# Delta rule of a two-block transformer: row spreads as one rounded product, pairs formed one ahead, the recurrence in halves of four heads

## The reference

```python
beta  = sigmoid(beta_logit)                       # per head and token
log_g = -exp(a_log) * softplus(decay_logit + dt_bias)
gam   = cumsum(log_g)                             # inside a chunk
decay = exp(gam[:, None] - gam[None, :])          # lower triangle, else 0
lower = strictly_lower(beta[:, None] * (k @ k.T) * decay)
T     = inverse(I + lower)
u_base, w_state = T @ (beta * v), T @ (beta * exp(gam) * k)
p_intra = (q @ k.T) * decay
q_dec, k_dec, g_tot = q * exp(gam), k * exp(gam[-1] - gam), exp(gam[-1])
for each chunk, with the state s of each head:
    u = u_base - w_state @ s
    o = q_dec @ s + p_intra @ u
    s = g_tot * s + k_dec.T @ u
```

## Time and profile before

| | us |
|---|---|
| median of 3 runs | 4046.73 |
| profiled execution, its time | 4045.87 |
| its span on the core | 4044.1 |
| PE busy (share of the span) | 3848.6 (95%) |
| DVE busy | 2100.2 (52%) |
| ACT busy | 1354.6 (33%) |

### The profile page before, as it was taken

One profiled execution on the slowest core, in us unless ns is written; L12 is line 12 of the kernel. 1 busy time (PEld: TensorE's weight loads), 2 busy tenths in 40 slices (PEclk: granted clock), 3 DMA queues, 4 the chain that ended last, 5 costly groups with the idle time before them and its releaser, 6 DMA issues.

```text
span 4044.1 us, 44571 instructions
## 1 busy us (share of the span) xinstructions
PE 3848.6 (95%) x18548; PEld 3142.1 (78%) x18548; DVE 2100.2 (52%) x3648; ACT 1354.6 (33%) x2046; POOL 86.1 (2%) x164
## 2 busy tenths in 40 slices
PE   8998989999999999999999988999999999799998
PEld 5974489999976688888877756888788877477886
DVE  5935757644466543343356467433633373756335
ACT  5434532221265332222237213222322264133222
POOL 0100001111000000000000000000000000000000
PEclk9997999999999999999999859999999999579999
DMA  6410014333220122232222101222222222002222
GB/s 225 145 42 1 1 47 136 128 123 128 92 73 11 58 94 99 94 112 99 94 88 84 58 1 42 99 96 97 86 99 95 99 79 83 1 27 84 99 94 84
DMA packets 92876, 333.34 MB, mean 82 GB/s; under 512 B 11362, under 2 KB 11522, under 8 KB 92420
## 3 DMA queue, kind: packets, MB, share of 16 engines
q1 hardware_dynamic: 77040, 278.10, 19.7%
q0 software_dynamic: 12800, 41.95, 3.3%
q10 hardware_dynamic: 2836, 10.44, 0.7%
HBM read 328.35 MB, written 2.10 MB: 82 GB/s over the span
## 4 chain that ended last, share of the span: by engine, by line
PE 90%; DVE 4%; ACT 4%; issue 1%; DMA 0%; DVEq 0%; ACTq 0%; SPq 0%
PE PS L510 73%; PE PS L1077 2%; PE PS L512 2%; PE PS L1062 1%; PE PS L1093 1%; PE PS L1065 1%; PE PS L1423 1%; PE PS L2122 1%; PE PS L1942 0%; PE PS L1943 0%; PE PS L943 0%; PE PS L1394 0%; PE PS L715 0%; PE PS L1960 0%; PE PS L2125 0%
## 5 line engine op out<-in xcount | busy, mean ns | idle before, releaser
L510 PE MATMUL PS<-arena_r,ring_hi 128*128 128x512 f32 (+1 forms) x6224 | 2103.9, 376 | 70.6 <-DVE H_r L679 70.1
L510 PE MATMUL PS<-arena_r,ring_r 128*128 128x512 f32 (+1 forms) x4752 | 1779.3, 374 | 0.0
L510 PEld LDWEIGHTS PS<-arena_r,ring_hi 128*128 128x128 f32 x6224 | 1166.8, 189 | 252.5 <-DVE H_r L679 61.2
L510 PE MATMUL PS<-H_r,ring_hi 128*128 128x512 f32 (+1 forms) x3280 | 1229.3, 375 | 0.0
L510 PEld LDWEIGHTS PS<-arena_r,ring_r 128*128 128x128 f32 x4752 | 896.3, 189 | 131.3
L379 DVE TENSOR_TENSOR ring_r<-ring,ring_hi 128x1024 fp32r<-128x1024 f32 x514 | 627.2, 1222 | 659.6 <-ACT ring_hi L370 658.8
L370 ACT ACTIVATE ring_hi<-ring 128x1024 fp32r<-128x1024 f32 x514 | 541.6, 1055 | 872.1 <-DMA ring<-weights_dram 864.1
L510 PEld LDWEIGHTS PS<-H_r,ring_hi 128*128 128x128 f32 x3280 | 621.5, 189 | 95.2 <-issue 3.1
L1653 ACT ACTIVATE arena<-PS 128x512 f32<-128x512 f32 x88 | 52.6, 598 | 533.5 <-PE PS L510 533.5
L1231 DVE SCALAR_TENSOR_TENSOR XH<-PS,mods,XH 128x256 f32<-128x256 f32 (+1 forms) x144 | 68.6, 524 | 238.0 <-PE PS L510 238.0
L1657 DVE SCALAR_TENSOR_TENSOR arena<-arena,PS 128x512 f32<-128x512 f32 x88 | 60.5, 687 | 224.8 <-PE PS L510 224.8
(11 more groups left out here) (362 smaller groups left out, 3199.1 us busy)
## 6 DMA issues: line engine op xcount, KB each, us to landing
ring<-weights_dram SPq DMA_DIRECT2D x526, 512.0 KB, 3.2
rstd<-ada_later_dram POOLq DMA_DIRECT2D x54, 256.0 KB, 2.9
mean<-ada_later_dram POOLq DMA_DIRECT2D x53, 256.0 KB, 3.0
ada_extra<-ada_later_dram POOLq DMA_DIRECT2D x53, 256.0 KB, 3.0
XH<-xT_dram ACTq DMA_DIRECT2D x1, 3072.0 KB, 20.1
ring<-weights_dram ACTq DMA_DIRECT2D x4, 512.0 KB, 3.9
out_dram<-XH SPq DMA_DIRECT2D x8, 256.0 KB, 2.0
con<-second_dram ACTq DMA_DIRECT2D x1, 1536.0 KB
```

The source lines that it names most:

```text
L510: ins = pe.matmul(PS[:, o.bank, 0:hi - lo], w[:, 0, :], x, **flags)
```

## The change

A row is split into a rounded high part (rows 0 to 7 of a tile of 40 rows) and the rest (rows 32 to 39), zeros between; the selectors `sel` and `selp` get ones at `r % 32`, so that one rounded product over 40 rows spreads high plus low part. Three sets of rows are split, beside the GEMM `in_plan`: `de`, beta and, new there, `exp(gam)` (`exp_row`), which leaves `rec_act`. `form` gives each of beta's spreads one of two banks, issues the spreads of pair p+1 before the k by q products of pair p, and DVE forms the arguments of pair p+1 before it weights pair p. `rec` spreads to the four output banks at once, and goes through each chunk in two halves g of four heads, with own semaphore steps and banks. DVE decays the state when `re_t` is there, no longer when `re_s` is.

```diff
-    for name, base, heads in (("self", 0, 4), ("selb", 32, 4), ("sel", 0, 8)):
+    a["sel"] = np.concatenate([np.broadcast_to(r % 32 == h, (P, P)) for h in range(8)], 1)
+    a["selp"] = np.concatenate([(r % 32 == 2 * p + c // 64) for p in range(4)], 1)
...
-            t[14]["beside_dve"] = lambda dve: l2_scale_dve(dve, 1)
+            t[14]["beside_dve"] = lambda dve: (l2_scale_dve(dve, 1), zero_rows_dve(dve, l))
...
-            t[15]["beside_act"] = turned_rows_act
+            t[15]["beside_act"] = lambda act: (turned_rows_act(act), high_rows_act(act))
...
-            t[17]["beside_dve"] = lambda dve: key_rows_dve(dve, l)
+            t[17]["beside_dve"] = lambda dve: (key_rows_dve(dve, l), low_rows_dve(dve))
...
             nc.scalar.activation(R4[0:8, :], be[0:8, :], ACT.Sigmoid).then_inc(gr_r4.sem, 1)
+            nc.scalar.activation(exp_row, de[0:8], ACT.Exp).then_inc(gr_r4.sem, 1)
...
+        def zero_rows_dve(dve, l):
+            if l == 0:
+                nc.vector.tensor_copy(con2_r[:, SEL:SEL + 1536], con2[:, SEL:SEL + 1536])
+            dve.wait_ge(gr_r4.sem, 2 * l + 2)
+            for _, t_r, at in row_splits:
+                ins = nc.vector.memset(t_r[at:at + 40].bitcast(F32), 0.0)
+            ins.then_inc(gr_zero.sem, 1)
+        def high_rows_act(act):
+            act.wait_ge(gr_zero.sem, gr_zero.next("act"))
+            for x, t_r, at in row_splits:
+                ins = nc.scalar.activation(t_r[at:at + 8], x, ACT.Copy)
+            ins.then_inc(gr_hi.sem, 1)
+        def low_rows_dve(dve):
+            dve.wait_ge(gr_hi.sem, gr_hi.next("dve"))
+            for x, t_r, at in row_splits:
+                nc.vector.tensor_tensor(t_r[at + 32:at + 40], x, t_r[at:at + 8].bitcast(F32), ALU.subtract)
+        def spread(pe, dst, name, at, rows, base=0):
+            at += SECOND_AT[name]
+            return pe.matmul(dst, con2_r[base:base + 40, at:at + P], rows[base:base + 40, :], start=True, stop=True)
...
         def form_pe(pe):
+            beta(0)
+            decays(0)
+            for p in range(4):
+                if p < 3:
+                    beta(p + 1)
                 pe.wait_ge(so_kb.sem, so_kb.at("pe", p))
+                if p >= 1:
+                    pe.wait_ge(so_lt.sem, so_lt.at("pe", 2 * p - 1))
+                products(p, 2, kbeta).then_inc(so_kk.sem, 1)
+                if p < 3:
+                    decays(p + 1)
+                if p >= 1:
+                    pe.wait_ge(so_L.sem, so_L.at("pe", 2 * p - 1))
+                products(p, 3, qkv).then_inc(so_kq.sem, 1)
...
         def form_dve(dve):
+            args(0)
+            for p in range(4):
+                if p < 3:
+                    args(p + 1)
+                weighted(p)
...
         def rec_pe(pe):
+            for g in range(2):
+                solved(0, g, vtok[:, 0, :])
             for p in range(4):
+                spread(pe, PS[:, 4 + p, :], "selp", P * p, exp_r, 64).then_inc(re_eg.sem, 1)
+            pe.wait_ge(re_gtx.sem, re_gtx.next("pe"))
             for n in range(4):
                 if n >= 1:
+                    for g in range(2):
+                        pe.wait_ge(re_sn.sem, re_sn.next("pe"))
+                        for p in (2 * g, 2 * g + 1):
+                            ins = pe.matmul(PS[:, 2 * g, P * (p - 2 * g):P * (p - 2 * g) + P], kbeta[:, p, cols], S[:, p, :],
+                                            start=True, stop=True)
+                        ins.then_inc(re_w.sem, 1)
                     for p in range(4):
+                        pe.matmul(PS[:, 4 + p, cols], S[:, p, :], qkv[:, p, cols], start=True, stop=False, skip_group_check=True)
+                    for g in range(2):
+                        pe.wait_ge(re_r.sem, re_r.next("pe"))
+                        solved(n, g, rr)
+                for g in range(2):
+                    pe.wait_ge(re_u.sem, re_u.next("pe"))
+                    if n < 3:
+                        for p in (2 * g, 2 * g + 1):
+                            ins = pe.matmul(PS[:, 1 + 2 * g, P * (p - 2 * g):P * (p - 2 * g) + P], ktok[:, n, P * p:P * p + P],
+                                            uu[:, P * p:P * p + P], start=True, stop=True)
+                        ins.then_inc(re_s.sem, 1)
+                if n == 0:
+                    pe.wait_ge(re_qd.sem, re_qd.next("pe", 4))
+                for g in range(2):
+                    for h in range(4 * g, 4 * g + 4):
+                        ins = pe.matmul(PS[half(h), 4 + h // 2, cols], uu[:, 64 * h:64 * h + 64], pt_of(h).chunk(n), start=(n == 0), stop=True,
+                                        skip_group_check=True)
+                    ins.then_inc(re_o.sem, 1)
...
         def rec_dve(dve):
+            for g in range(2):
+                for p in (2 * g, 2 * g + 1):
+                    dve.wait_ge(re_eg.sem, re_eg.next("dve"))
+                    nc.vector.tensor_tensor(qkv[:, p, :], qkv[:, p, :], PS[:, 4 + p, :], ALU.mult)
+                    nc.vector.tensor_tensor(kbeta[:, p, :], kbeta[:, p, :], PS[:, 4 + p, :], ALU.mult).then_inc(re_qd.sem, 1)
+                decay_state(0, g)
+                update_state(0, g)
+            for n in range(1, 4):
+                for g in range(2):
+                    dve.wait_ge(re_w.sem, re_w.next("dve"))
+                    nc.vector.tensor_tensor(rr[:, 256 * g:256 * g + 256], vtok[:, n, 256 * g:256 * g + 256], PS[:, 2 * g, 0:256],
+                                            ALU.subtract).then_inc(re_r.sem, 1)
+                for g in range(2):
+                    decay_state(n, g)
                 if n < 3:
+                    for g in range(2):
+                        update_state(n, g)
```

More of the change, by code:

```diff
@@ L2112, in program, with beta, decays @@
             "solve_y64_copied", "solve_off64", "solve_off64_copied"))
+        so_lt, so_kq = signal("solve_L_weighted"), signal("solve_query_products")
         def form_pe(pe):
[L2115 to L2118, removed]
+            def beta(p):
+                if p >= 2:
+                    pe.wait_ge(so_kb.sem, so_kb.at("pe", p - 2))
+                spread(pe, PS[:, 4 * (p % 2), :], "selp", P * p, mean_r).then_inc(so_beta.sem, 1)
+            def decays(p):
@@ L2119, in form_pe, with products @@
                 for s in range(2):
                     if p >= 1:
-                        pe.wait_ge(so_L.sem, so_L.at("pe", 2 * p - 2 + s))
-                    pe.matmul(PS[:, 1 + 4 * s, :], C("sel", P * (2 * p + s))[0:8], de[0:8, :], start=True, stop=True)
+                        pe.wait_ge(so_arg.sem, so_arg.at("pe", 2 * p - 2 + s))
+                    ins = spread(pe, PS[:, 1 + 4 * s, :], "sel", P * (2 * p + s), be_r)
+                ins.then_inc(so_in.sem, 1)
+            def products(p, bank, of):
@@ L2133, in form_pe @@
-                ins.then_inc(so_kk.sem, 1)
+                        ins = pe.matmul(PS[:, bank + 4 * s, P * n:P * n + P], qkv[half(s), 4 + p, P * n:P * n + P],
+                                        of[half(s), p, P * n:P * n + P], start=True, stop=True)
+                return ins
+            beta(0)
[3 more added lines that the diff above has]
+                    beta(p + 1)
+                pe.wait_ge(so_kb.sem, so_kb.at("pe", p))
+                if p >= 1:
[6 more added lines that the diff above has]
+                products(p, 3, qkv).then_inc(so_kq.sem, 1)
@@ L2134, in form_pe @@
             so_kb.advance("pe", 4)
+            so_arg.advance("pe", 8)
+            so_lt.advance("pe", 8)
             so_L.advance("pe", 8)
@@ L2309, in rec_pe @@
[L2309 to L2323, removed]
-                    act.wait_ge(re_o.sem, re_o.at("act", n - 1))
-                nc.scalar.activation(uu, PS[:, 3 if n == 0 else 2, :], ACT.Copy).then_inc(re_u.sem, 1)
-            re_o.advance("act", 4)
@@ new lines, in rec_pe, with rec_act @@
+                if n == 0:
+                    pe.wait_ge(re_qd.sem, re_qd.next("pe", 4))
+                for g in range(2):
+                    for h in range(4 * g, 4 * g + 4):
+                        ins = pe.matmul(PS[half(h), 4 + h // 2, cols], uu[:, 64 * h:64 * h + 64], pt_of(h).chunk(n), start=(n == 0), stop=True,
+                                        skip_group_check=True)
+                    ins.then_inc(re_o.sem, 1)
+        def rec_act(act):
+            act.wait_ge(re_gt.sem, re_gt.next("act"))
+            nc.scalar.activation(gtot, PS[:, 1, 0:16].rearrange("p (q n) -> p q n", q=4), ACT.Exp).then_inc(re_gtx.sem, 1)
+            for n in range(4):
+                for g in range(2):
+                    act.wait_ge(re_t.sem, re_t.next("act"))
+                    if n >= 1:
+                        act.wait_ge(re_o.sem, re_o.at("act", 2 * n - 2 + g))
+                    nc.scalar.activation(uu[:, 256 * g:256 * g + 256], PS[:, 2 * g, 256:512], ACT.Copy).then_inc(re_u.sem, 1)
+            re_o.advance("act", 8)
```

112 lines of the change are left out of this document (47 added, 65 removed).

## The result

The changed kernel takes 4013.1 us in the median (4012.0 to 4016.5, 4 runs) against 4046.7 for the kernel before: a ratio of 0.9917, 95% interval 0.9901 to 0.9932. The forecast was 4019, 6 us too high. The profiled execution took 4012.0 us (span 4009.9).

A forecast was written before the change was run, and what follows sets the result against it. TensorE, 90% of the span, was taken as the bound, with time saved where it waits or runs slowly. Per layer -11.7 - 5.7 + 1.9 + 1.7 = -13.8 us, twice -27.6, gives 4019; range 4007 to 4031.

The forecast's parts named there:

- The spreads: In `form`, a rounded spread over 40 rows takes 0.43 us in the slow clock, against 1.86 for float32.
- `form`: Stage `form` goes from 38.1 to 26.4 us, -11.7 per layer, with pairs of 6.5 us in the slow clock.
- rival (a): In `form` the fast clock holds: 22.5 us instead of 26.4, total 4011; chance 0.11.
- `rec`: Stage `rec` goes from 40.8 to 35.1 us, -5.7 per layer; chunk 1 starts at 13.8, chunks take 5.9.
- The table switch: In `in_plan` the added exponential makes ACT switch tables; PE waits 4.3 instead of 2.36 us, +1.9 per layer.
- The clock behind that wait: In `in_plan`, after PE's 4.3 us wait, the clock falls to half for 3.5 us, +1.7 per layer.
- Taken at nothing: In `in_plan`, clears, cast, high and low parts behind the wait cost 0 to 0.7 us, taken as 0.
- `solve` unchanged: Stage `solve` keeps its time, with no term in the sum.
- (b): In `form` and `rec` nothing overlaps, only cheaper spreads pay: -8.3 us per layer, total 4030; chance 0.10.
- (c): In `rec` the fast clock never comes: stage 49.1 us, +0.2 per layer, total 4047; chance 0.05.
- (d): In `in_plan` the longer wait drops the clock until the stage's end, up to 70 us per layer, 4155; chance 0.02.

The follow-up runs named there:

- run 2: Changed kernel with `form` in the new order but its spreads float32 products over 8 rows again: 4034.7 us, ratio 0.9969.
- run 1: Changed kernel with `form` going through its pairs in the old order, keeping only the rounded spreads: 4018.7 us, ratio 0.9925.
- runs 3 and 4: Changed kernel with `rec`'s chunks through 8 heads at once: first with the state decayed only after the update (4023.6 us), then with the early decay (4021.2 us).
- Runs 5 and 6: Changed kernel with 18 unread products filling PE's wait in `in_plan` (4013.0 us); changed kernel with the new exponential behind the last roots on ACT (4005.8 us).
- run 7: Changed kernel with the new exponential behind the last roots, and the turns of the rows and what follows a tile later: 4007.1 us, ratio 0.9908.
- run 9: run 7 with the roots and new exponential a tile later on ACT (3998.6 us), plus unread products where PE waits in `form`: 3999.3 us.

## Why the prediction was right, point by point

- **The spreads** (0.43 us taken for a step): right. Single records of 0.62 and 0.77 us in `form`; the four in `rec` stand in 2.07 us, with steps of 0.43 between the last three.
- **`form`** (26.4 us, pairs of 6.5, slow clock): right in the first layer, 26.0 with pairs of 6.43. In the second the clock came back for part of it and it took 25.0, between the forecast and rival (a). That the loop runs through the spreads also in the new order is shown by run 2; that both parts are needed, by runs 1 and 2 together.
- **`rec`** (35.1; chunk 1 at 13.8, chunks of 5.9, copies from 32.6): 34.8; 13.5, 5.93 and 32.3. The half-width operation taken at 0.4 us took 0.42. The clock was back at 16 to 17 us as before the change, in the changed kernel and in runs 3 and 4.
- **The table switch** (+1.9, wait of 4.3): the two ACT instructions took 1.96 us and the wait grew by 2.13, to 4.49. The function starts 0.02 us behind its load, so the drain that the Trainium skill ("ScalarE: Activation LUTs", section "What ACT_TABLE_LOAD costs") adds isn't seen here either.
- **The clock behind that wait** (+1.7): right, 1.6. Runs 5 and 6 show that it was this wait: no fall behind 0.41 and 2.38 us, a fall behind 4.49. Its length alone doesn't decide, since in run 7 the clock fell behind 1.78 us in the first layer and stayed full behind the same 1.78 us in the second.
- **Taken at nothing** (clears, cast, high and low parts): right. `high_rows_act` waited 4.35 us for the clears, and PE did not wait behind that.
- **`solve` unchanged**: the one step that failed. Its code is the same, but it took 1.5 us less in the first layer and 1.0 in the second, since the full clock at `form`'s end now lasted 1.5 and 1.8 us into it. In the first layer DVE's wait of 1.94 us became 0.54, which is nearly all of it. That the clock is the reason rests on the rows of ten kernels; no run changed it alone. Nothing in the forecast says so, and this part of the gain is luck.
- **The 6 us missed:** the spans of the two profiled executions differ by 34.2 us, 6.6 more than forecast. Of these, 2.5 come from `solve`, 1.9 from `form` (0.4 and, beyond a forecast of -11.7, 1.5 in the second layer) and 0.4 from `rec`; `in_plan` cost 0.2 more than forecast. The other 2.0 lie in code ahead of and behind these stages that the change leaves alone; their cause is open.
- **Rivals:** (b) is refuted by the changed kernel's pairs and chunks, (c) by its clock in `rec`, (d) by its steps of 0.23 us from 2218.9 on. (a) happened in part, in the second layer.

## What to carry to other kernels

A new order of the work pays only after the slowest link of the loop is short: measured alone it gave 0.5 us, behind the cheaper spreads 4.1. A small function put on a full ACT queue is priced by its place: behind a function of another table it cost 3.7 us a layer on PE, behind one of the same table nothing. Before a wait is moved, look at what stands behind the late work on the same queue: moving PE's turn gained nothing until ACT's order was moved with it.

## What the runs showed of the hardware that was not expected

PE busy for 19.4 of 20.1 us (run 9, first layer) was granted half clock all along, while the same code was granted full clock for most of the last 12 us of the loop in the second layer (mean 0.85). A wait of 1.78 us was followed by half clock in one layer of run 7 and not in the other. A stretch of full or half clock runs on over the border of two stages: unchanged code in `solve` took 87.2 to 92.3 us, and DVE's two waits of 1.9 and 1.3 us behind PE are part of that. Single executions of one kernel can lie further apart than these effects: in run 1 one took 4001.9 us and the other three 4018.6 to 4019.9, and in run 2 the seven lie between 4020.0 and 4037.8. A difference of a few us between two of them therefore says little; rows of the stage do.
